# Fourier mixing over folded tokens: cosines and sines contract over 256 rows each in a two-block transformer kernel

## What is computed

```python
FOURIER_GROUPS = 8           # 8 groups of 64 features, BRANCH_WIDTH = 512

def fourier_mix(a):
    b, s, _ = a.shape
    g = a.reshape(b, s, FOURIER_GROUPS, FOURIER_GROUP_DIM).transpose(0, 2, 1, 3).astype(F32)
    f = jnp.real(jnp.fft.fft2(g, norm='ortho'))
    return f.transpose(0, 2, 1, 3).reshape(b, s, BRANCH_WIDTH).astype(a.dtype)

def first_block(x, ...):
    for layer in range(DEPTH):               # DEPTH = 2
        u = rms_norm(x, norm_mix_g[layer])
        proj = jnp.einsum('bsd,de->bse', u, w_in[layer])
        (a_in, bq, bk, bv, cq, ck, cv, co, cgate, dq, dk, dv, gates) = split_cols(proj)
        y_a = fourier_mix(a_in)
        ...
```

## Time and profile before

| | |
|---|---|
| median of 3 runs | 3653.83 us |
| lowest and highest | 3651.8, 3656.82 us |
| time of the profiled execution | 3656.83 us |
| its span, first to last instruction | 3655.5 us |
| granted TensorE clock, mean (1 is 2.4 GHz) | 0.981 |
| busy: TensorE, DVE, ACT, POOL | 96%, 40%, 37%, 36% of the span |
| instructions | 39205 |

### The profile page before, as it was taken

How to read it: one execution, slowest core, us unless ns; L and a number is a source line. 1 busy time by engine, 2 the same in 40 slices (tenths; PEclk the granted TensorE clock), 3 DMA queues, 4 the chain that set the end, 5 groups by cost and what they waited for, 6 DMA issues and landing times.

```text
span 3655.5 us, 39205 instructions
## 1 busy us (share of the span) xinstructions
PE 3515.7 (96%) x14412; PEld 2601.9 (71%) x14412; DVE 1459.8 (40%) x2796; ACT 1367.3 (37%) x2605; POOL 1320.1 (36%) x1016
## 2 busy tenths in 40 slices
PE   8999999999999999999999989988899999789999
PEld 5556776787787755667677778864588886468887
DVE  3432457444324243255644352355422124542212
ACT  2343334533223244333544322345433234543222
POOL 1222333344444322323244534430144443025444
PEclk9999999999999999999999999998999999899999
DMA  4111112233323211112123322210033322013333
GB/s 159 52 67 55 58 64 65 69 98 122 99 95 96 64 52 47 63 55 70 58 77 111 111 81 94 97 64 24 31 110 104 97 95 81 12 41 104 98 98 104
DMA packets 154751, 286.80 MB, mean 78 GB/s; under 512 B 17980, under 2 KB 20061, under 8 KB 154432
## 3 DMA queue, kind: packets, MB, share of 16 engines
q1 hardware_dynamic: 153232, 281.90, 23.9%
q10 hardware_dynamic: 1328, 2.39, 0.2%
HBM read 278.85 MB, written 5.37 MB: 78 GB/s over the span
## 4 chain that ended last, share of the span: by engine, by line
PE 83%; DVE 9%; ACT 5%; issue 2%; POOL 2%; DMA 0%; ACTq 0%; POOLq 0%; DVEq 0%
PE bank L508 23%; PE bank L510 22%; PE bank L509 22%; PE bank L566 3%; DVE work L1425 2%; POOL wl L2035 2%; PE bank L707 2%; PE bank L625 2%; PE bank L575 1%; ACT wh L969 1%; DVE work L1376 1%; PE bank L742 1%; PE bank L756 1%; PE bank L754 1%; PE bank L933 1%
## 5 line engine op out<-in xcount | busy, mean ns | idle before, releaser
L2035 POOL TENSOR_TENSOR wl<-raw,wh 128x512 fp32r<-128x512 f32 x1012 | 1319.9, 1317 | 2323.7 <-ACT wh L969 2100.0
L508 PE MATMUL bank<-Uh,wh 128*128 128x512 f32 x2720 | 1144.4, 421 | 36.5 <-POOL wl L2035 22.3
L510 PE MATMUL bank<-Uh,wl 128*128 128x512 f32 x2720 | 1068.9, 393 | 0.0
L509 PE MATMUL bank<-Ul,wh 128*128 128x512 f32 x2720 | 1067.5, 392 | 0.0
L969 ACT ACTIVATE wh<-raw 128x512 fp32r<-128x512 f32 x1012 | 601.8, 621 | 641.3 <-PE bank L510 621.3
L508 PEld LDWEIGHTS bank<-Uh,wh 128*128 128x128 f32 x2720 | 515.1, 189 | 255.0 <-issue 117.6
L509 PEld LDWEIGHTS bank<-Ul,wh 128*128 128x128 f32 x2720 | 516.3, 190 | 123.0 <-issue 23.0
L510 PEld LDWEIGHTS bank<-Uh,wl 128*128 128x128 f32 x2720 | 514.6, 189 | 112.0
L1376 DVE TENSOR_TENSOR work<-bank,rs 128x512 f32<-128x512 f32 x308 | 212.8, 691 | 895.1 <-PE bank L510 857.8
L508 PE MATMUL bank<-Hh,wh 128*128 128x512 f32 x1258 | 503.1, 400 | 9.0 <-ACT work L1060 5.9
L510 PE MATMUL bank<-Hh,wl 128*128 128x512 f32 x1258 | 490.4, 390 | 0.0
(11 more groups left out here) (206 smaller groups left out, 2841.5 us busy)
## 6 DMA issues: line engine op xcount, KB each, us to landing
raw<-in_units SPq DMA_DIRECT2D x1012, 256.0 KB, 2.8
work<-in_dft SPq DMA_DIRECT2D x6, 512.0 KB, 9.4
xT<-in_xT SPq DMA_DIRECT2D x8, 256.0 KB, 9.2
scratch<-work SPq DMA_DIRECT2D x1, 2048.0 KB, 7.7
out<-xT SPq DMA_DIRECT2D x8, 256.0 KB, 2.9
table<-scratch SPq DMA_DIRECT2D x4, 448.0 KB, 5.1
work<-in_dft SPq DMA_DIRECT2D x2, 640.0 KB, 11.3
scratch<-table SPq DMA_DIRECT2D x1, 1152.0 KB, 5.3
```

Source lines behind the costliest of these rows:

```text
L508: nc.tensor.matmul(out, H, xh, start=k == 0, stop=False)
L509: nc.tensor.matmul(out, H, xl, start=False, stop=False)
L510: mm = nc.tensor.matmul(out, L, xh, start=False, stop=k == x.kt - 1)
L2035: nc.gpsimd.tensor_tensor(g.wl[:, a:a + PK * P], g.raw[:, a:a + PK * P], g.wh[:, a:a + PK * P].bitcast(F32), ALU.subtract).then_inc(g.s_lo, 1)
```

## The change

The token matrices are folded. For tile p, DVE forms the sums a[j] + a[S - j] and the differences a[j] - a[S - j] for j = 1 to 255 (`fold_tokens`), column 0 is copied, and token 256 is kept in a tile `zero` that holds zeros otherwise. The folded tile has sums in its first 256 columns, differences in its last 256. The feature transform then takes cosines for the first two blocks of 128 and sines for the last two, each a matmul of 128 columns, and a fifth matmul adds token 256 to the free first row of the third block. One DVE copy instead of two takes the result to SBUF. The token transform has four matmuls instead of eight. The tables shrink to cosines and sines of 256 tokens, with row 0 of the first sine block replaced by the cosine row of token 256.

```diff
         finish_of(i, "a", 1)
         beat(i, "F", 1)
-        pe.wait_ge(g.landed["dft"], 16 * 4 * (l + 1))
+        pe.wait_ge(g.landed["dft"], 16 * 5 * (l + 1))
 
         def fourier_features(p):
-            a = w(p % 2)
-            pe.wait_ge(s_dve, at("V", "ev", i, "a", p))
-            for half in range(2):
-                b = (2 if p % 2 == 0 else 6) + half
-                take(b, s_dve, "V", "feat", i, p, half)
-                for j in (2 * half, 2 * half + 1):
-                    mm = nc.tensor.matmul(bank[b][:, (j % 2) * 2 * P:(j % 2 + 1) * 2 * P], a[:, j * P:(j + 1) * P],
-                                          w(16)[:, 0:2 * P], start=True, stop=True)
-                mm.then_inc(s_pe, T("feat", i, p, half))
+            even, zero = w(13 + p % 2), w(15)[:, (p % 2) * P:(p % 2 + 1) * P]
+            b, col = (2 if p % 2 == 0 else 6), w(12)
+            pe.wait_ge(s_dve, at("V", "fold", i, p))
+            take(b, s_dve, "V", "feat", i, p)
+            for j in range(NT):
+                out, half = bank[b][:, j * P:(j + 1) * P], col[:, (j // 2) * P:(j // 2 + 1) * P]
+                mm = nc.tensor.matmul(out, even[:, j * P:(j + 1) * P], half, start=True, stop=j != 2)
+                if j == 2:
+                    nc.tensor.matmul(out, zero, col[:, 0:P], start=False, stop=True)
+            mm.then_inc(s_pe, T("feat", i, p))
 
         def fourier_tokens(p):
-            pe.wait_ge(s_dve, at("V", "feat", i, p, 1))
-            b = 4 + p % 2
+            pe.wait_ge(s_dve, at("V", "feat", i, p))
+            b, f = 4 + p % 2, w(2 + p % 2)
             take(b, s_dve, "V", "H", i, 0, p)
-            f = 2 + 2 * (p % 2)
             for j in range(NT):
-                for cs in range(2):
-                    x = f * S + j * 2 * P + cs * P
-                    mm = nc.tensor.matmul(bank[b][:, :], g.work[:, x:x + P], w(8 + 4 * cs + j),
-                                          start=j == 0 and cs == 0, stop=j == NT - 1 and cs == 1)
+                mm = nc.tensor.matmul(bank[b][:, :], f[:, j * P:(j + 1) * P], w(8 + j), start=j == 0, stop=j == NT - 1)
             mm.then_inc(s_pe, T("y", i, p))
...
+    def fold_tokens(i, t):
+        a, out, zero = w(t % 2), w(13 + t % 2), w(15)[:, (t % 2) * P:(t % 2 + 1) * P]
+        h = S // 2
+        if t < 2:
+            nc.vector.memset(zero, 0.0).then_inc(s_dve, V())
+            nc.vector.memset(out[:, h:h + 1], 0.0).then_inc(s_dve, V())
+        else:
+            dve.wait_ge(s_pe, at("T", "feat", i, t - 2))
+        settle()
+        nc.vector.tensor_copy(zero[:, 0:1], a[:, h:h + 1]).then_inc(s_dve, V())
+        nc.vector.tensor_copy(out[:, 0:1], a[:, 0:1]).then_inc(s_dve, V())
+        nc.vector.tensor_tensor(out[:, 1:h], a[:, 1:h], a[:, S - 1:h:-1], ALU.add).then_inc(s_dve, V())
+        nc.vector.tensor_tensor(out[:, h + 1:S], a[:, 1:h], a[:, S - 1:h:-1], ALU.subtract).then_inc(
+            s_dve, V("fold", i, t))
...
                 leave(i, x, g.landing(i, x), "ev", i, kind, t, scale=scale)
+                if kind == "a":
+                    fold_tokens(i, t)
...
         def features(p):
-            f = 2 + 2 * (p % 2)
-            for half in range(2):
-                b = (2 if p % 2 == 0 else 6) + half
-                dve.wait_ge(s_pe, at("T", "feat", i, p, half))
-                if p >= 2:
-                    dve.wait_ge(s_pe, at("T", "y", i, p - 2))
-                nc.vector.tensor_copy(w(f + half), bank[b][:, :]).then_inc(s_dve, V("feat", i, p, half))
+            dve.wait_ge(s_pe, at("T", "feat", i, p))
+            if p >= 2:
+                dve.wait_ge(s_pe, at("T", "y", i, p - 2))
+            nc.vector.tensor_copy(w(2 + p % 2), bank[2 if p % 2 == 0 else 6][:, :]).then_inc(s_dve, V("feat", i, p))
...
     def transforms():
-        edges = [0, 2 * S, 4 * S, 6 * S, 8 * S + 2 * P]
-        for a, b in zip(edges, edges[1:]):
-            nc.sync.dma_start(g.work[:, 8 * S + a:8 * S + b], A["dft"][:, a:b]).then_inc(landed["dft"], 16)
+        dft = A["dft"]
+        nc.sync.dma_start(w(8, 2), dft[:, 0:2 * S]).then_inc(landed["dft"], 16)
+        nc.sync.dma_start(w(10)[1:P, :], dft[1:P, 4 * S:5 * S]).then_inc(landed["dft"], 16)
+        nc.sync.dma_start(w(10)[0:1, :], dft[0:1, 2 * S:3 * S]).then_inc(landed["dft"], 16)
+        nc.sync.dma_start(w(11), dft[:, 5 * S:6 * S]).then_inc(landed["dft"], 16)
+        nc.sync.dma_start(w(12)[:, 0:2 * P], dft[:, 8 * S:8 * S + 2 * P]).then_inc(landed["dft"], 16)
```

## The result

| | before | changed |
|---|---|---|
| median | 3655.23 us | 3633.41 us |
| lowest and highest | 3651.8, 3656.82 (4 runs) | 3629.77, 3635.75 (4 runs) |
| profiled execution, span | 3656.83, 3655.5 us | 3629.77, 3628.1 us |
| granted TensorE clock, mean | 0.981 | 0.982 |

The kernel became faster: ratio 0.9941, interval 0.9925 to 0.9957, 21.8 us less. I had forecast 31.2 us less. The direction held, the size did not: 9.4 us of the gain are missing, and the time is 2.4 us over the top of my range. Of the 10.9 us between my 3622.5 and 3633.41, 1.4 are the kernel before itself, whose median is 3655.23 over four runs and was 3653.83 over the three that I had.

What follows compares the result with a forecast made beforehand. TensorE was taken to bound the kernel. Terms of -27.5 (token transform), -5.0 (feature transform), +0.3 (fold waits) and +1.0 (`spread2` stall) gave -31.2 us, 3622.6 from the 3653.83 median, rounded to 3622.5; range 3616 to 3631 us.

Steps and rivals of the forecast that it cites:

- What bounds the kernel: Whole kernel and Fourier stage: TensorE bounds the stage alone, so removing TensorE work is worth what it removes.
- Token transform: Fourier stage, `L625`: per tile 8 matmuls become 4, 3.43 us less for each of 8 tiles, 27.5 us less.
- Feature transform: Fourier stage, `L613`: ten records of 0.11 us replace eight, 1.1 us against 1.73 per tile, 5.0 us less.
- rival of the weight loads: Feature blocks: weight loads of 190 ns hold ten records to 1.9 us a block; 3629.0 us, chance 8%.
- The folds: DVE behind `a` evictions: 0.43 us per sum at forward price; a clash with POOL's splits can stretch a fold to 4.0.
- slow fold: DVE fold: a backward operand costs several times the forward price; 3671 us at 5 us a sum; slower 3%, even 1 to 2%.
- 0.3 us for waits at the features: Before the feature blocks of p = 0 and 1: TensorE waits for folds, 0.3 us more, bounds 0 and 2.7.
- The `spread2` stall: Layer 0, tile 0: the fold delays the first `spread2` copy, TensorE idles 0.5 to 1.1 us; taken as 1.0 more.
- The DMA step: Table loads: four transfers become five, needed only later; priced at nothing unless a landing took more than twice as long.
- The late clock: Opening of layer 0: the new stall delays TensorE's clock rise, costing 2.1 to 4.5 us; 3627.1 us, chance 7%.
- The gain taken back behind the stage: Behind the Fourier stage: TensorE's wait hangs on something that does not move, a layer's 16 us go; 3638.2 us, 5%.

Runs made afterwards that it cites:

- packed kernel: Changed kernel with its transform tables laid out contiguously by the host and loaded by two transfers of 128 rows each; 3626.17 us, ratio 0.992.
- 127 rows late: Changed kernel with the 127-row transfer issued behind the `scratch1` write and two weight pieces in the opening, behind the other tables in the second load; 3626.61 us.
- kernel before with 127 rows: Kernel before, nothing folded, with half of its second table transfer issued as 127 rows and 1 row, the other half by itself; 3669.92 us, ratio 1.0041.
- 112 and 15 rows: Changed kernel with only its 127-row table transfer split, into one of 112 and one of 15 rows; 3626.01 us, ratio 0.992.
- The fold placed later: Changed kernel with tables in two 128-row transfers and, in layer 0, the fold of tile 0 behind the six `spread2` copies; 3622.25 us, ratio 0.9903.

## Why the prediction was right and where it was wrong

**What bounds the kernel.** Right: the stages are TensorE's alone, before and after.

**Token transform.** Right: blocks of 3.43 us, as taken.

**Feature transform.** Right within 0.02 us a block: 1.12 us for ten records against the 1.1 I took from four records elsewhere. Both stages together gave 32.05 us of the 32.5. The rival of the weight loads (1.9 us a block) fell.

By the 81 ns a pair that the Trainium skill states ("TensorE: Matmul & The Clock Gate", "Back-to-back issue gap") a block would be an estimated 0.8 us long; no row shows that, ten records took 1.12.

**The folds.** The forward price of 0.43 was right for the backward operand too (0.41), and the slow fold, my rival on the slower side, fell. The clash with POOL's splits is there as feared, 1.08 to 1.50 us for one sum of a fold, and its cover held everywhere but at the `spread2` blocks: the 0.3 us for waits at the features was nothing.

**The `spread2` stall.** The mechanism was right, the size was not: 1.67 us where I took 1.0 and at most 1.1. My working took the blocks as 0.93 us each, half of it 0.46 a pass, "where it still runs at the lower of its two clock levels". But 0.46 was the mean over twelve passes at two levels. In the packed kernel the first four blocks last 2.85 us at the high level, where 0.93 each gives 3.7; all twelve passes at the low level take 8.05 us in the changed kernel, 0.67 a pass. So the fifth block is due 0.9 us earlier than I had it, and the stall is longer. What the stall is worth in the time of the kernel is not shown: the features start at 51.09 to 54.66 in the runs that have it and no late landing, and at 51.73 in the one without. The row of one group with one mean hid it; the clock by stretches, shown above for the kernel before, would have told it.

**The DMA step: this failed.** I wrote "Price nothing; only if a landing took more than twice as long would it count". I asked when TensorE needs the tables, and that answer held (127 rows late, no cost). I didn't ask what is queued behind them. I had counted SP's issues and put the uneven one down as a transfer like the others, though my own sentence named it: "one of a single row and one of 127 rows". Behind it came the write to `scratch1` and two weight pieces, and for the first of these ACT, and through it TensorE, waits in the opening. It cost 7.9 to 8.0 us, by three kernels on one chip. Against the packed kernel, the traces of the changed one place 5.5 and 6.9 us of this before the first features and 0.7 and 0.3 at the second load; the rest lies in parts that scatter by more. The same step on the second load, "a whole feed-forward ahead", failed in the same way: in the kernel before with 127 rows that load cost 5.2 us. Forecast less this term: 31.2 less 8.0 is 23.2, against 21.8 measured.

**The rest.** Cured of it, the kernel is 29.8 us faster (packed) and 29.9 (112 and 15 rows) than before, 1.4 short of the forecast. By the terms, 0.45 are the stages and 0.7 the stall, if it counts in full, less 0.3 for waits that didn't come; the rest is within the scatter of the parts that no edit touched. The range should have held an uneven transfer as a case of its own.

**The late clock.** In kind it came true, from another cause: the clock did stay at 0.50 until 56 us, but after 5.26 us of idle time for a landing, not after the short stall. For the stall itself the rival stays open. With the same 1.67 us the features start at 52.05 in the packed kernel, no later than the 52.21 before, but at 53.17 with the late 127 rows and at 54.66 without the fifth matmul.

**The gain taken back behind the stage.** It fell: 5.11 us of idle time, and the part between the stages is 0.01 us off.

## What to carry to other kernels

Before a transfer is cut to other rows, look whether its count of rows still spreads over all DMA engines; 127 rows went through one of them, while 112 and 15 cost nothing that shows. A transfer that nobody waits for yet is not free: list what is issued behind it, on its queue and on the same DMA engines, and ask when that is needed, for each place in the program where the transfer is made. And where a group of instructions spans a change of clock, don't divide its time by its count.

## What was not expected of the hardware

- One DMA engine moved 25 to 27 GB/s here, where all together moved 300 to 421. The issue that shows the delay is not the uneven one (0.34 us) but the next (12.65 us).
- TensorE's clock fell while it was busy without a gap. In the kernel before it read 1.00 from 36 to 40 us, 0.75 from 40 to 44 and 0.50 from 44 to 48, and TensorE was busy for all of each stretch, with the `spread2` matmuls of 33 rows by 384 columns. The fold placed later shows the same, 0.69 and 0.50 with 4.00 of 4.00 busy. Why it fell was not tried.
- Reading an SBUF operand backwards costs DVE nothing that can be seen: 0.41 us for 255 columns, with a forward operand beside it, and by the straight line from forward operations 0.43.
